# Five weight remainders of VectorE moved to later places in the head loop of a hybrid attention and expert layer

## The chip, the cores and the metric

One Trainium2 chip, one of its cores. The metric is the device time of one execution in microseconds (us), lower is better. The kernel before was timed three times: 2218.05, 2221.12 and 4329.31 us, median 2221.12 us. All operands are float32.

## The reference

One layer on 256 tokens of width 2048. The part that matters here is the first third: an RMS norm, one wide input projection, and three mixers of eight heads of width 128 each, all read from that projection.

```python
xn = rms_norm(x, mix_norm[i])
proj = xn @ w_in[i]
(aq, ak, av, bq, bk, bv, c_qkv, c_a, c_b, c_z, g_a, g_b, g_c) = jnp.split(proj, split_at, axis=-1)
out_a = sliding_window_sink_attention(...)   # softmax over two chunks of 64, with a sink
out_b = stick_breaking_attention(...)        # blocks of 128
# out_c: gated delta rule in chunks of 64. The inverse of (I - N) by squaring:
for _ in range(int(math.log2(CHUNK)) - 1):
    power = power @ power
    t_mat = t_mat + t_mat @ power
# then a recurrence over the chunks: v_new = u - w @ state; state = state * decay + k^T v_new
```

Behind it come the gates and the branch projections (merged output, then `w_out`), a mixture of 32 experts with top-2 routing, and a gated per-layer embedding.

## The kernel before, in words

**Weights in two parts.** Every float32 product with a large weight is done in three passes of fp32r matmuls. ScalarE rounds a landed weight tile to its high part (`wh = copy(slot)`, in `hi`), VectorE computes the remainder (`wl = slot - wh`, in `lo`, line 1332 in the heads and line 1529 for the units of the gate stage), and TensorE adds `wh·xh`, `wh·xl` and `wl·xh`. `lo` begins with a wait for its `hi` (semaphore `w_hi`) and ends by raising `v_lo`.

**Tiles and slots.** A head needs eight tiles of the projection (q, k, v of the delta net, v, q, k of stick-breaking, z of the delta net, q of the window attention), each 2048 x 128, 1 MB. Four slots of the ring hold them. The sync engine issues the load of tile t+4 into the slot of tile t once TensorE has finished tile t (`tile_mm`, line 306). `wl` overwrites the slot in place, `wh` has its own four buffers.

**The head loop.** While head n is mixed, TensorE computes the tiles of head n+1. This is written out by hand: `mix(m, n, dense)` on TensorE (line 529) calls `dense(q)` for q = 0 to 31 between the small matmuls of the mixing; four calls make a tile of 48 matmuls, 12 in a call (`bank<-xh,wh`, `xl,wh`, `xh,wl` in the rows, line 492). The third pass, which needs `lo` of its tile, starts at the ninth matmul of the third call of a tile (wait at line 489). Tile s is thus `dense(4s)` to `dense(4s+3)`. The loop runs seven times; the eighth head is mixed after it with the first units of the gates in place of the tiles, where `lo(2)`, `lo(3)`, `lo(5)`, `lo(6)` and `lo(9)` do units 2, 3, 4, 5, 6 and 7, and `lo(4)`, `lo(7)` and `lo(8)` nothing.

**Order on TensorE around the change.** After `dense(12)` it waits for the softmax weights (`sw_pr`) and transposes them (line 591). Then six rounds r = 0 to 5 of the inverse: `dense(13+r)`, the last matmul of which is held until VectorE and ScalarE have copied the results of the round before (`dn_round`, `dn_roundp`), then small matmuls of 64x64 (lines 600, 603 or 605, and 610). Then `dense(19)`, lines 626 and 628, `dense(20)`, line 632 (the off-diagonal block, `dn_x`), `dense(21)`, line 637 (first half of the new values, which needs the copied block, `dn_inv`), line 638, `dense(22)`, `dense(23)`, line 642 (needs the first half copied, `dn_vn`), `dense(24)`, `dense(25)`, line 648 (needs the state copied), `dense(26)`, `dense(27)`, line 654 (needs the second half copied), and `dense(28)` to `dense(31)`.

**Order on VectorE.** `mix` (from line 1418) is one in-order queue. The lines of the change: the minimum for stick-breaking (1471), the sum, reciprocal and products of the softmax weights (1473 to 1478), the round copies (1482, 1484; 1488 in the last round) each with a tap of the next head's convolution behind it in rounds 0 to 3 (1407, 1409), the product with z (1495), the copy of the off-diagonal block (1497), of the first half of the new values (1500), the SiLU of the next head (1415), the copy of the state (1503) and of the second half (1506). These short steps stand between `lo(2)` to `lo(9)`. `lo(4)` to `lo(7)` make the remainders of the tiles 4 to 7 of the next head, `lo(8)` and `lo(9)` those of the tiles 0 and 1 of the head after it.

**Order on ScalarE.** Round copies of the other operand of the squaring (`dn_roundp`), with `hi(5)` ahead of the rounds, `hi(6)` behind the copy of round 3, the sigmoids of z and of the convolution behind the copy of round 4, `hi(7)` behind the copy for line 638, `hi(8)` behind `evac(5)` after it. In the last head `hi(5)` and `hi(6)` round units 4 and 5.

Of the kernel before, what the change touches and what calls it, by code (L numbers as in the profile page):

```python
# [81 lines left out]
def hybrid_trunk(nc, x, p, mix_norm, w_in, swa_q_norm, swa_k_norm, swa_sinks, sb_q_norm, sb_k_norm, dn_conv,  # L82
# [3 lines left out]
    with ctx:  # L86
# [22 lines left out]
        def sem(name):  # L109
            name = base.get(name, (name, 0))[0]  # L110
            if name not in sems:
                sems[name] = ctx.enter_context(nc.semaphore(name))
            return sems[name]

        def event(name, n):

            name, before = base.get(name, (name, 0))
            return sem(name), n + before
# [861 lines left out]
        def bc(ap, shape):  # L980
            return ap.to_broadcast(shape)
# [321 lines left out]
        def _(dve):  # L1303
            tt, ts, stt = dve.tensor_tensor, dve.tensor_scalar, dve.scalar_tensor_tensor

            def nxt():

                dve.drain()  # L1308
# [20 lines left out]
            def lo(p, t):  # L1329

                dve.wait_ge(*event("w_hi", t + 1))
                tt(wl[p][:], slot[p], wh[p][:], ALU.subtract).then_inc(sem("v_lo"), 1)  # L1332
# [84 lines left out]
            def mix(n, next_tap, next_silu, lo):  # L1417
                one = ds(n - 1, 1)
                dve.drain()
                dve.tensor_copy(hs[:], head[:, 0:F_CONV, one].rearrange("p f a -> p (f a)"))  # L1420
                dve.tensor_copy(v_sw, vt_sw[:, ds((n - 1) // 4, 1), :].rearrange("p a s -> p (a s)"))
                nxt()

                dve.wait_ge(*event("sb_rt", n))
                stt(qk_sb[:, 0:S], raw_sb[:, 0, :], gains[:, 5:6], r_sb[:, 0:S], ALU.mult, ALU.mult)
                stt(qk_sb[:, S:2 * S], raw_sb[:, 1, :], gains[:, 3:4], r_sb[:, S:2 * S], ALU.mult, ALU.mult)\
                    .then_inc(sem("sb_qk"), 1)
                dve.wait_ge(*event("dn_rt", n))
                stt(qk_dn[:, 0:S], cv[:, 0:S], HS, r_dn[:, 0:S], ALU.mult, ALU.mult)
                tt(qk_dn[:, S:2 * S], cv[:, S:2 * S], r_dn[:, S:2 * S], ALU.mult).then_inc(sem("dn_qk"), 1)  # L1430

                G = Gb[:, one, :].rearrange("p a s -> p (a s)")
                for t in range(TT):
                    i = stt(decT[:, t * P:t * P + P], G[:, t * P:t * P + P], hs[:, F_NGC + t:F_NGC + t + 1], capdn,
                            ALU.add, ALU.min)
                i.then_inc(sem("dn_diff"), 1)
                lo(2)
                dve.wait_ge(*event("sw_rt", n))
                stt(q_sw, raw_sw, gains[:, 6:7], r_sw, ALU.mult, ALU.mult).then_inc(sem("sw_q"), 1)

                dve.wait_ge(*event("sb_ln", n))
                stt(sp, bank[3][:, 0:384], 0.0, za, ALU.max, ALU.add)
                nxt()
                spd = sp.rearrange("p (b n) -> p b n", b=3)[:, 0:3:2, :]
                tt(spd, spd, bc(upper[:].unsqueeze(1), [P, 2, P]), ALU.mult).then_inc(sem("sb_sp"), 1)
                lo(3)

                dve.wait_ge(*event("sw_s", n))
                tt(smx, bank[4][:, 0:384], masksw[:].rearrange("p b n -> p (b n)"), ALU.add)
                nxt()  # L1450
                dve.tensor_reduce(sm[:, 0:1], smx[:, 0:P], AX.X, ALU.max)
                dve.tensor_reduce(sm[:, 1:2], smx[:, P:3 * P], AX.X, ALU.max)
                nxt()
                ts(sm[:, 2:4], sm[:, 0:2], hs[:, F_SINK:F_SINK + 1], -1.0, ALU.max, ALU.mult).then_inc(sem("sw_max"), 1)

                dve.wait_ge(*event("dn_dec", n))
                dve.wait_ge(*event("dn_kk", n))
                tt(attnT, bank[7][:, S:2 * S], decT, ALU.mult)
                tt(decT, bank[7][:, 0:S], decT, ALU.mult)
                nxt()  # L1460
                tt(nT, decT.rearrange("p (t n) -> p t n", t=TT), nBb[:, one, :].rearrange("p a (t n) -> p (a t) n", t=TT),
                   ALU.mult).then_inc(sem("dn_round"), 1)
                nxt()
                for i, rows_ in enumerate(BLOCKS):
                    tt(powT[rows_, :, 1, :], nT[rows_, :, CH * i:CH * i + CH],
                       bc(ident[rows_, CH * i:CH * i + CH].unsqueeze(1), [CH, TT, CH]), ALU.add)
                dve.wait_ge(*event("dn_eg", n))
                tt(eG, eG, qk_dn[:, P:S], ALU.mult).then_inc(sem("decays_used"), 1)
                lo(4)
                dve.wait_ge(*event("sb_arg", n))  # L1470
                tt(am, bank[3][:, 0:384], capsb[:].rearrange("p b n -> p (b n)"), ALU.min).then_inc(sem("sb_amin"), 1)
                dve.wait_ge(*event("sw_exp", n))
                tt(sm[:, 8:10], sm[:, 4:6], sm[:, 6:8], ALU.add)
                nxt()
                dve.reciprocal(sm[:, 10:12], sm[:, 8:10])
                nxt()
                ts(smx[:, 0:P], smx[:, 0:P], sm[:, 10:11], None, ALU.mult)
                ts(smx[:, P:3 * P], smx[:, P:3 * P], sm[:, 11:12], None, ALU.mult).then_inc(sem("sw_pr"), 1)
                for r in range(6):
                    dve.wait_ge(*event("dn_sqr", 6 * n - 5 + r))  # L1480
                    if r < 5:
                        i = dve.tensor_copy(powT[:, :, 0, :], pow_psum[:, :, 0, :])
                        if r:
                            i = tt(powT[:, :, 1, :], pow_psum[:, :, 1, :], powT[:, :, 1, :], ALU.add)  # L1484
                        i.then_inc(sem("dn_round"), 1)
                    else:
                        for j, rows_ in enumerate(BLOCKS):
                            i = tt(inv[rows_, :, CH * j:CH * j + CH], pow_psum[rows_, :, 1, :], powT[rows_, :, 1, :], ALU.add)
                        i.then_inc(sem("dn_T"), 1)
                    if r < 4:  # L1490
                        next_tap(r)
                    if r in (1, 3):
                        lo(5 + r // 2)
                dve.wait_ge(*event("z_sig", n))
                tt(ez, ez, raw_z, ALU.mult).then_inc(sem("dn_sz"), 1)
                dve.wait_ge(*event("dn_x", n))
                dve.tensor_copy(inv[BLOCKS[0], :, CH:P], x_psum).then_inc(sem("dn_inv"), 1)
                lo(7)
                dve.wait_ge(*event("dn_v", 2 * n - 1))
                dve.tensor_copy(vn[:, 0:P], bank[6][:, 0:P]).then_inc(sem("dn_vn"), 1)  # L1500
                next_silu()
                dve.wait_ge(*event("dn_ds", n))
                dve.tensor_copy(state, bank[2][:, S:S + P]).then_inc(sem("dn_state"), 1)
                lo(8)
                dve.wait_ge(*event("dn_v", 2 * n))
                dve.tensor_copy(vn[:, P:S], bank[6][:, P:S]).then_inc(sem("dn_vn"), 1)
                dve.wait_ge(*event("dn_ort", n))
                tt(r_dn[:, 0:S], r_dn[:, 0:S], ez, ALU.mult)
                nxt()
                stt(outs[:, 2, one, :].rearrange("p a s -> p (a s)"), bank[4][:, 0:S], gains[:, 4:5], r_dn[:, 0:S],  # L1510
                    ALU.mult, ALU.mult).then_inc(sem("head"), 1)
                lo(9)
# [11 lines left out]
            with dve.Fori(1, NH) as h:  # L1524
                mix(h, lambda j: tap(j, h + 1), lambda: silu(h + 1), lambda s: lo(s % PAIRS, 8 * h + s + PRO))
# [5 lines left out]
            def first_units(s):  # L1531
                for u in {2: (2,), 3: (3,), 5: (4,), 6: (5,), 9: (6, 7)}.get(s, ()):
                    unit_lo(u)

            mix(NH, lambda j: None, lambda: None, first_units)

            def prod(i):
# [278 lines left out]
```

## Time and profile before

| | |
|---|---|
| runs | 2218.05, 2221.12, 4329.31 us; median 2221.12 |
| profiled execution | 2226.76 us, its span 2224.6 us |
| mean granted TensorE clock | 0.936 |
| TensorE busy | 1822.3 us, 82% of the span |
| VectorE busy | 893.1 us, 40% |
| ScalarE busy | 691.5 us, 31% |
| DMA queue of the sync engine | 592.19 MB, 71.5% of 16 engines |

Stages, in us from the start of the span: up to 138.5 the norms, the first tiles and the masks; 138.5 to 643.2 the seven turns of the head loop; 643.2 to 700 the last head; 700 to 1075 gates and branches; to 1215 the output projection and the router; to the end the experts and the embedding. In the seven turns TensorE is busy 456.9 of 504.7 us and the DMA engines 43% of the time; in the last stage the DMA engines are busy 95%.

How to read it: a row of the timeline gives the start, the time taken, the engine, the line and the operation, how many in a row, and in brackets how long the engine had been idle before it and who released it. Matmuls are pipelined, so that a row begins before the one ahead of it has ended: distances are best taken from start to start.

### The profile page before, as it was taken

Reading aid. Unit: us, or ns where it says so; the run is one execution under the profiler, and the core shown is the slowest. Engines: PE = TensorE matmul, PEld = TensorE weight load, DVE = VectorE, ACT = ScalarE, POOL = GpSimd, SP = SyncE. Lnnn points to the kernel's source line nnn. Section 1 sums busy time; section 2 is a strip of 40 time slices with the busy share of each in tenths; the row PEclk is TensorE's granted clock in tenths of the full one; section 3 lists DMA queues with packets and bytes.
Section 4 is the critical chain, followed back from the end, with each engine's and each line's share of the span. In section 5 each row is a group of like instructions: output and inputs, shape, how many; then the busy total and the mean of one; then the engine's idle time right before and its main releaser. Section 6 shows DMA issues by size and latency. Waiting matters only on the chain.

```text
span 2224.6 us, 42071 instructions
## 1 busy us (share of the span) xinstructions
PE 1822.3 (82%) x17850; PEld 1371.7 (62%) x17851; DVE 893.1 (40%) x1420; ACT 691.5 (31%) x952; POOL 26.4 (1%) x40
## 2 busy tenths in 40 slices
PE   5999889999988999999896776666666666666799
PEld 5888888888866888888774443333333333333367
DVE  2464455445544454544443233222222222222274
ACT  3355446554554333333332111001001101011063
POOL 4000000000000000000000000000000000000000
PEclk8999999999998999999998999988988998988899
DMA  8454434544423556555675999999999999999972
GB/s 160 131 135 115 127 98 113 132 113 111 115 94 114 190 189 197 191 197 189 259 274 236 415 427 425 426 426 425 426 426 427 426 427 426 426 427 425 426 273 101
DMA packets 258897, 593.00 MB, mean 267 GB/s; under 512 B 31514, under 2 KB 171034, under 8 KB 225306
## 3 DMA queue, kind: packets, MB, share of 16 engines
q1 hardware_dynamic: 258842, 592.19, 71.5%
q8 instruction: 43, 0.70, 0.1%
q14 instruction: 12, 0.10, 0.0%
HBM read 590.07 MB, written 2.10 MB: 266 GB/s over the span
## 4 chain that ended last, share of the span: by engine, by line
PE 49%; DMA 33%; ACT 6%; DVE 4%; issue 3%; SPq 2%; DVEq 1%; ACTq 1%
DMA ring<-in_w_e_down 32%; PE bank L694 21%; PE bank L492 11%; PE bank L875 4%; PE bank L933 4%; ACT wh L987 3%; PE bank L848 2%; DVE wl L1332 2%; ACT ring L987 2%; SPq L296 1%; DVEq L1308 1%; ACT L987 1%; PE bank L834 1%; DMA ring<-in_w_in 1%; PE bank L894 1%
## 5 line engine op out<-in xcount | busy, mean ns | idle before, releaser
L987 ACT ACTIVATE wh<-ring 128x2048 fp32r<-128x2048 f32 x156 | 298.3, 1912 | 255.4 <-DMA ring<-in_w_in 130.8
L848 PE MATMUL bank<-ring,mo 128*32 128x128 f32 x6144 | 215.2, 300 | 138.5 <-DMA ring<-in_w_e_up 116.5
L848 PEld LDWEIGHTS bank<-ring,mo 128*32 128x32 f32 x6144 | 186.6, 121 | 182.1 <-DMA ring<-in_w_e_up 146.0
L1529 DVE TENSOR_TENSOR wl<-ring,wh 128x2048 fp32r<-128x2048 f32 x86 | 197.2, 2293 | 237.2 <-ACT wh L987 237.1
L987 ACT ACTIVATE mo<-bank 128x128 f32<-128x128 f32 (+2 forms) x145 | 47.7, 335 | 649.3 <-PE bank L862 310.3
L875 PE MATMUL bank<-ring,mo 128*32 128x512 f32 x1024 | 164.0, 772 | 89.4 <-DMA ring<-in_w_e_down 84.6
L1332 DVE TENSOR_TENSOR wl<-ring,wh 128x2048 fp32r<-128x2048 f32 x68 | 155.4, 2287 | 57.5 <-ACT wh L987 57.5
L492 PE MATMUL bank<-xh,wh 128*128 128x256 f32 x1088 | 168.1, 304 | 3.5 <-ACT xh L987 3.5
L492 PE MATMUL bank<-xl,wh 128*128 128x256 f32 x1088 | 161.6, 296 | 3.9 <-POOL xl L448 3.9
L1698 DVE TENSOR_TENSOR x_tok<-x_tok,bank 128x512 f32<-128x512 f32 x256 | 158.2, 680 | 0.0
L492 PE MATMUL bank<-xh,wl 128*128 128x256 f32 x1088 | 148.9, 286 | 6.8 <-DVE mo L1484 6.8
L492 PEld LDWEIGHTS bank<-xh,wh 128*128 128x128 f32 x1088 | 144.7, 199 | 12.6 <-issue 5.3
L492 PEld LDWEIGHTS bank<-xl,wh 128*128 128x128 f32 x1088 | 145.6, 199 | 7.3 <-POOL xl L448 4.2
L875 PEld LDWEIGHTS bank<-ring,mo 128*32 128x32 f32 x1024 | 34.0, 126 | 185.1 <-DMA ring<-in_w_e_down 94.7
L492 PEld LDWEIGHTS bank<-xh,wl 128*128 128x128 f32 x1088 | 137.6, 192 | 8.6 <-DVE mo L1484 8.2
L1708 DVE COPY mo<-bank 128x512 f32<-128x512 f32 x32 | 22.1, 692 | 238.7 <-PE bank L834 238.7
L1722 DVE TENSOR_TENSOR mo<-mo,bank 128x128 f32<-128x128 f32 x32 | 9.2, 288 | 270.5 <-PE bank L848 270.5
L987 ACT ACTIVATE raw_dn<-bank 128x512 f32<-128x512 f32 (+1 forms) x56 | 28.0, 500 | 252.2 <-PE bank L875 245.4
L694 PE MATMUL bank<-wh,xl 128*128 128x512 f32 x384 | 100.6, 401 | 5.0 <-DVE mo L1484 5.0
L694 PE MATMUL bank<-wh,xh 128*128 128x512 f32 x384 | 98.8, 397 | 2.5 <-ACT ring L987 2.3
L987 ACT ACTIVATE ring<-bank 128x128 f32<-128x128 f32 (+6 forms) x132 | 47.8, 378 | 168.3 <-PE bank L610 56.9
L987 ACT ACT_TABLE_LOAD x66 | 84.7, 1283 | 44.4 <-issue 43.2
(352 smaller groups left out, 2319.1 us busy)
## 6 DMA issues: line engine op xcount, KB each, us to landing
ring<-in_w_e_down SPq DMA_DIRECT2D x64, 2048.0 KB, 26.1
ring<-in_w_e_up SPq DMA_DIRECT2D x64, 2048.0 KB, 26.3
ring<-in_w_in SPq DMA_DIRECT2D x116, 1024.0 KB, 5.5
ring<-in_w_e_gate SPq DMA_DIRECT2D x32, 2048.0 KB, 30.6
xnT<-in_w_e_gate SPq DMA_DIRECT2D x16, 2048.0 KB, 29.9
mo<-in_w_e_gate SPq DMA_DIRECT2D x16, 2048.0 KB, 34.2
ring<-in_w_out SPq DMA_DIRECT2D x16, 1024.0 KB, 5.3
ring<-in_w_ple_gate SPq DMA_DIRECT2D x8, 2048.0 KB, 15.3
```

Source lines behind the costliest of these rows:

```text
L296: sp.dma_start(to, of).then_inc(sem("small_in"), 16)
L492: m = mm(to, w_[:, k, :], x_[:, k, :], start=(i == 0), stop=(i == len(steps) - 1))
L694: m = mm(to[t][:], x_(k0 + k, t), w_[p][:, k, :], start=(first and j < 8 and k == 0), stop=(last and j >= 16 and k == 3))
L834: m = mm(bank[0][32 * j:32 * j + 32, :], selw[:, t, :], h_rows[:, t, 512 * j:512 * j + 512], start=(t == 0), stop=(t == 1))
L848: m = mm(bank[b][32 * j:32 * j + 32, 0:P], xw[:, 8 * (i % 2) + k, :], m_gu[piece][:, k, j * P:j * P + P], start=(i % 2 == 0 and k == 0), s ...
L875: m = mm(bank[3][32 * j:32 * j + 32, :], hT[:, 32 * c:32 * c + 32], m_down[i][:, 0, a, j * 512:j * 512 + 512], start=(c == 0), stop=(c == 3))
L894: m = mm(bank[t][:], kT_sw[:, j, t * P:t * P + P], wpp[:, j, ds(n * 512, 512)], start=(j == 0), stop=(j == 1))
L933: m = mm(bank[ACC_BANK[u // 2] + t][:], x_[:, 8 * (u % 2) + k, t * P:t * P + P], w_[:, k, :], start=(first and k == 0), stop=(last and k = ...
L987: return act.activation(out, in_, func, **kw)
L1332: tt(wl[p][:], slot[p], wh[p][:], ALU.subtract).then_inc(sem("v_lo"), 1)
L1529: tt(ul[u % PAIRS], unit_slot[u % PAIRS], uh[u % PAIRS], ALU.subtract).then_inc(sem("u_lo"), 1)
L1698: i = tt(o, o, bank[4 + j][:], ALU.add)
```

## The change

In `mix` of VectorE five calls of `lo` move. `lo(4)` goes from ahead of the stick-breaking minimum to behind the softmax weights. `lo(5)` and `lo(6)` leave the rounds 1 and 3 of the inverse: `lo(5)` goes behind the product with z, `lo(6)` to the place of `lo(7)`, behind the copy of the off-diagonal block. `lo(7)` goes to the place of `lo(8)`, behind the copy of the state, and `lo(8)` behind the copy of the second half of the new values. Their order among themselves, what they compute, and every other engine's program stay.

```diff
                 tt(eG, eG, qk_dn[:, P:S], ALU.mult).then_inc(sem("decays_used"), 1)
-                lo(4)
                 dve.wait_ge(*event("sb_arg", n))
...
                 ts(smx[:, P:3 * P], smx[:, P:3 * P], sm[:, 11:12], None, ALU.mult).then_inc(sem("sw_pr"), 1)
+                lo(4)
                 for r in range(6):
...
                     if r < 4:
                         next_tap(r)
-                    if r in (1, 3):
-                        lo(5 + r // 2)
                 dve.wait_ge(*event("z_sig", n))
                 tt(ez, ez, raw_z, ALU.mult).then_inc(sem("dn_sz"), 1)
+                lo(5)
                 dve.wait_ge(*event("dn_x", n))
                 dve.tensor_copy(inv[BLOCKS[0], :, CH:P], x_psum).then_inc(sem("dn_inv"), 1)
-                lo(7)
+                lo(6)
                 dve.wait_ge(*event("dn_v", 2 * n - 1))
                 dve.tensor_copy(vn[:, 0:P], bank[6][:, 0:P]).then_inc(sem("dn_vn"), 1)
                 next_silu()
                 dve.wait_ge(*event("dn_ds", n))
                 dve.tensor_copy(state, bank[2][:, S:S + P]).then_inc(sem("dn_state"), 1)
-                lo(8)
+                lo(7)
                 dve.wait_ge(*event("dn_v", 2 * n))
                 dve.tensor_copy(vn[:, P:S], bank[6][:, P:S]).then_inc(sem("dn_vn"), 1)
+                lo(8)
                 dve.wait_ge(*event("dn_ort", n))
```

## Rows read from the trace of the kernel before

**Rows 1.** Waits of TensorE in the head loop: total us, times, longest us

```profile
PE bank L591 <- DVE ring L1478: 18.9, 7, 2.7
PE bank L642 <- DVE mo L1500: 12.8, 7, 1.8
PE bank L492 <- DVE mo L1484: 6.8, 7, 1.0
PE bank L541 <- ACT ring L987: 6.6, 7, 1.6
```

**Rows 2.** Timeline of the fifth turn, around the softmax weights

```profile
439.02 2.28 DVE L1332 TENSOR_TENSOR wl<-ring,wh 128x2048 fp32r<-128x2048 f32 x1
441.23 0.55 DVE L1471 TENSOR_TENSOR ring<-bank,capsb 128x384 f32<-128x384 f32 x1
...
442.36 0.35 DVE L1478 TENSOR_SCALAR ring<-ring,sm 128x256 f32<-128x256 f32 x1
...
442.76 0.55 PE L591 MATMUL bank<-ident,ring 128*128 128x128 f32 x3 [2.69 <-DVE ring L1478]
...
445.39 0.29 DVE L1482 COPY mo<-bank 128x128 f32<-128x128 f32 x1 [2.68 <-PE bank L610]
```

**Rows 3.** Timeline of the fifth turn, rounds 3 to 5 of the inverse

```profile
451.46 1.92 PE L492 MATMUL bank<-xh,wh 128*128 128x256 f32 x12
...
456.36 2.29 DVE L1332 TENSOR_TENSOR wl<-ring,wh 128x2048 fp32r<-128x2048 f32 x1 [0.25 <-ACT wh L987]
456.56 1.22 PE L492 MATMUL bank<-xl,wh 128*128 128x256 f32 x8
...
456.68 0.28 ACT L987 ACTIVATE ring<-bank 128x128 f32<-128x128 f32 x1 [0.36 <-PE bank L610]
...
458.27 0.42 ACT L987 ACTIVATE mo<-mo 128x256 f32<-128x256 f32 x1
...
459.10 0.38 PE L492 MATMUL bank<-xh,wl 128*128 128x256 f32 x1 [0.96 <-DVE mo L1484]
459.42 0.45 PE L605 MATMUL bank<-mo,ring 64*64 64x64 f32 x8
459.79 1.70 PE L492 MATMUL bank<-xh,wl 128*128 128x256 f32 x12
```

**Rows 4.** Timeline of the fifth turn, from the block to the first half

```profile
463.65 0.44 PE L632 MATMUL bank<-ring 64*64 64x64 f32 x4
...
465.56 0.39 PE L637 MATMUL bank<-mo 128*128 128x128 f32 x2
...
466.38 1.91 ACT L987 ACTIVATE wh<-ring 128x2048 fp32r<-128x2048 f32 x1
...
468.32 2.29 DVE L1332 TENSOR_TENSOR wl<-ring,wh 128x2048 fp32r<-128x2048 f32 x1 [3.91 <-ACT wh L987]
...
470.87 0.49 PE L642 MATMUL bank<-mo,ring 128*128 128x128 f32 x2 [1.83 <-DVE mo L1500]
```

**Rows 5.** Windows: length, busy us (count) of PE, PEld, DVE, ACT, POOL; clock, DMA

```profile
442.76:459.42 16.66, 15.69 (x164) 14.10 (x164) 11.31 (x24) 9.18 (x17) 0.00 (x0) 1.00 0.28 73
514.89:533.05 18.16, 17.19 (x163) 15.32 (x163) 11.31 (x24) 9.29 (x16) 0.00 (x0) 0.91 0.26 68
544.51:547.93 3.42, 3.42 (x28) 3.42 (x29) 3.21 (x3) 0.39 (x1) 0.00 (x0) 1.00 1.04 285
470.87:475.79 4.92, 4.92 (x29) 4.92 (x30) 3.21 (x3) 0.39 (x1) 0.00 (x0) 0.65 0.72 198
673.50:683.90 10.40, 10.37 (x38) 7.20 (x39) 1.58 (x5) 0.65 (x2) 0.00 (x0) 0.52 0.01 2
708.00:1060.00 352.00, 349.35 (x1554) 289.19 (x1552) 171.03 (x103) 135.62 (x91) 0.00 (x0) 1.00 0.59 192
```

**Rows 6.** Timeline of the last head, round 4 of the inverse

```profile
670.66 0.26 ACT L987 ACTIVATE ring<-bank 128x128 f32<-128x128 f32 x1
...
673.53 0.79 PE L694 MATMUL bank<-wh,xl 128*128 128x512 f32 x1 [5.05 <-DVE mo L1484]
```

## The prediction, as it was written before the changed kernel ran

> **What bounds the kernel now.** I read the windows first. The change touches only the head loop and the last head, 138.5 to 700 us of the span, and there TensorE is nearly always busy while VectorE and the DMA engines are not half so. So I asked the waits of TensorE in the loop what its gaps are [rows 1]: the reader is to see that the three longest are all for VectorE, seven times each, once a turn: 2.7 us for the softmax weights, 1.8 us for the first half of the new values, 1.0 us for a round of the inverse. The fourth, for ScalarE's inverse root, is no part of the change. Then the timeline of one turn shows what VectorE does just before it releases TensorE, and each time it is a remainder of 2.28 or 2.29 us, which nobody needs yet [rows 2 to 4]. Last, windows of the same stretches in different turns show what the gaps do to TensorE's clock [rows 5], and the last head is read apart [rows 6]. All starts below are those of the fifth turn; the gaps repeat to 0.02 us in the other six.
>
> **The change part by part.** Nothing is computed anew: eight remainders a turn before and after. Each term is a gap of TensorE that ends earlier.
>
> *lo(4), ahead of the minimum.* VectorE starts it at 439.02, the minimum at 441.23, and the softmax weights are done at 442.36 + 0.35 = 442.71, 1.48 us after the minimum began [rows 2]. TensorE has been idle since 442.76 - 2.69 = 440.07. With the remainder gone the minimum starts at 439.02, the weights are there at 440.50, and TensorE starts at 440.54: 0.47 us of the gap stays, 2.22 us go. Behind the weights the remainder runs from about 440.4 to 442.7. What is next on VectorE's queue is the copy of round 0, at 445.39 now, 443.17 then, and it was idle 2.68 us ahead of it [rows 2]: 0.5 us of cover is left, so this place costs nothing; without the cover it would delay round 0, whose result TensorE holds its twelfth matmul for, over a microsecond later. ScalarE's exponential of the minimum only comes earlier.
>
> *lo(5), in round 1.* It ends 1 us into the next stretch of twelve matmuls and holds back the last of it: that stretch takes 1.92 us where one after 64-wide matmuls takes 1.70 when nothing holds it [rows 3]. 0.22 us go.
>
> *lo(6), in round 3.* It waits for `hi(6)`, starts at 456.36, and the copies of round 4 come after it. TensorE's twelve matmuls start at 456.56 and line 605 at 459.42: 2.86 us, of which 0.96 is a gap and the rest of the surplus the slow restart. Not held, they take 1.63 to the next start (0.07 less than the 1.70 of the row at 459.79, whose end overlaps what follows). ScalarE's copy for the same round is there at 456.96, so it does not take VectorE's place. 2.86 - 1.63 = 1.23 us go.
>
> *lo(5) in its new place* starts behind the product with z. That one needs the sigmoid, done at 458.27 + 0.42 = 458.69 less the 0.22 from above [rows 3], and the copies of round 5, which end about 1.1 us after line 605; line 605 starts at 456.56 - 0.22 + 1.63 = 457.97. So the product ends at 459.5, the remainder at 461.7. The block that VectorE must copy next comes out of line 632, which starts 4.23 us after line 605 [rows 3, 4], hence at 462.2, and ends at 462.6. 0.9 us of cover: cost nothing. If the cover were gone, the copy could still be 1.3 us late before line 637, a dozen matmuls on, waits.
>
> *lo(6) in its new place* runs from 462.9 to 465.1 (`hi(6)` is long done). Line 637 starts 6.14 us after line 605 [rows 3, 4], at 464.1, so VectorE copies the first half at 465.1 to 465.4, about 0.9 us later than it could. Line 642 waits for it. It could have started at 470.87 - 1.83 = 469.04 [rows 4], 9.62 us after line 605, in the new turn at 467.6. 2.2 us of cover, cost nothing.
>
> *lo(7), ahead of the first half.* It had to wait for `hi(7)`, which starts at 466.38, because that stands behind line 638 on ScalarE; it starts at 468.32 and makes line 642 late by 1.83 us, plus a slow first matmul, 0.49 against 0.22 us [rows 4]. 2.10 us go. Behind the state's copy it finds `hi(7)` done, runs 2.3 us, and the second half comes about 3.0 us after that copy: 0.7 us of cover, and then 24 matmuls before line 654 needs the copy of it. *lo(8)* behind that copy has nothing queued behind it but the output, for which VectorE idles for over ten microseconds. Each costs nothing.
>
> *Remainders as TensorE needs them.* The third pass of tile 5 starts 16 matmuls ahead of the end of `dense(23)`, 2.1 us before 467.6; lo(5) is done at 461.7, 3.8 us ahead. The others have 7 us or more. No DMA is issued by VectorE, and the loads of the sync queue wait for TensorE's tiles, not for remainders; they are shifted with the tiles.
>
> Sum of a turn: 2.22 + 0.22 + 1.23 + 2.10 = 5.77 us; times seven, **40.4 us**.
>
> *The clock.* In some turns TensorE runs for 3.4 us at the lower of its two levels (1.2 in place of 2.4 GHz) right after one of the two long gaps. From line 591 to 605 a turn takes 16.66 us at a granted clock of 1.00 and 18.16 at 0.91; from 642 to 648 it is 3.42 at 1.00 and 4.92 at 0.65 [rows 5]. Five turns have it in the first stretch and three in the second: 8 x 1.50 = 12.0 us. It comes back if the gaps of 2.69 and 1.83 us are what lowers the clock. For that speaks that none of the eight comes after the gap at line 541, 6.6 / 7 = 0.9 us [rows 1], and that the gates, without such gaps, run 352 us at 1.00 [rows 5]. Bounds: nothing comes back, or all of it does. I take all of it, since gaps of 0.5 and 0.9 us are what remains. The Trainium skill has a rule against this ("TensorE: Matmul & The Clock Gate", A second HAM failure mode): short idle times between groups of matmuls, if frequent, make the clock swing between its levels. By it the small gaps that remain would keep the stretches, and the sum would be 12 us less.
>
> *The last head.* lo(5) and lo(6) are units 4 and 5 there. TensorE is idle 5.05 us until VectorE's round 4, behind the remainder of unit 5. ScalarE's copy for that round is itself behind `hi` of unit 5, which waits for its load, and is done at 670.92 [rows 6]. So the gap ends at about 671.0 and not at 673.53: 2.5 us go. The next 10.4 us run at 0.52 [rows 5], 5.1 us dearer than at full clock; between none and all of it I take a third, 1.7 us, since half the gap stays. Together **4.2 us** (2.5 to 7.6).
>
> All of it: 40.4 + 12.0 + 4.2 = 56.6 us. The profiled execution took 2226.76 us, its span 2224.6, so it would be 2170.2. The median of the runs is 5.6 us lower; 2221.12 - 56.6 = 2164.5, taken as **2165 us**, -2.5%.
>
> **The rivals.** *A, the clock keeps swinging* (the skill's rule; 0.13). For it: its low stretches are short and stand wherever a turn has gaps. Against: rows 5. The eight stretches and the last head's stay: 2165 + 12.0 + 1.7 = 2179 us.
>
> *B, a moved remainder becomes a new wait* (0.14). The tightest places have 0.5 (round 0) and 0.9 us (the block) of cover, and VectorE is one queue. If the block's copy or round 0 ends up behind a whole remainder in each turn, TensorE waits at line 637 or in `dense(14)`: up to 2.3 us x 7 = 16 us back, 2181 us.
>
> *C, the remainders come too late for the third pass* (0.03), the case on the slower side. Its place is the wait at line 489; its price is the whole remainder exposed, 5 x 2.29 x 7 = 80 us, less the 57: 2244 us. It decides only once lo(5) is more than 3.8 us later than I have it and the others over 7. Against it: every `hi` stands unchanged on ScalarE, and is done before the new place.
>
> *D, the gain is given back later* (0.05): the experts are bound by the DMA engines, and would absorb what comes sooner if their loads ran on a clock of their own: 2221 us. Against: their first loads wait for units of the output projection, so they shift with TensorE. That the change does not do what it says is in the same 0.05: the calls are the same on one in-order queue, so I see no way to it.
>
> **How the numbers follow.** Forecast 2165 us with 0.65. Its own spread is 2150 (all of the last head's clock, the fastest run of 2218 as the base, and the scatter of a run) to 2176 (half of the clock). Range 2150 to 2186, which takes in A, B and a part of both together; C, D and the tails are left out, under 0.2. A difference of 2% (44 us, about what a measurement can tell) means below 2177. Forecast 0.62, a third of A and a quarter of B: 0.70 faster. Within 2%: 0.28. Slower by over 2%: 0.02, as even C stays at +1%.
>
> **What would show it.** In the trace after: the gap at line 591 about 0.5 us; no gap at line 642 and none at line 492 released by 1484; a turn of 64.5 to 65 us in place of 72.1; clock 1.00 in the loop; 2.5 us of gap in the last head's round 4. The prediction is wrong if TensorE waits at 637 or 489, if the copy at 1482 of round 0 starts right on the end of a remainder with TensorE held, if the clock still shows eight stretches at half, or if the experts start no earlier than 50 us before.

## The result, and the profile after

The changed kernel takes 2167.64 us (median of 4 runs, 2164.89 to 2171.17) against 2220.61 us before: a ratio of 0.9766, 95% interval 0.9746 to 0.9787, faster. One of the four runs of the kernel before took 4329.31 us and is not in the ratio. Forecast were 2165 us and 2150 to 2186. The profiled execution took 2164.89 us, its span 2162.8.

The waits of TensorE in the seven turns of the head loop and the start of the last head (total us, times, longest us), which answer to [rows 1]:

```profile
PE bank L541 <- ACT ring L987: 5.0, 6, 0.8
PE bank L591 <- DVE ring L1477: 3.4, 7, 0.5
PE bank L534 <- ACT ring L987: 1.2, 1, 1.2
```

The rows for line 642 and for the rounds are gone, the one for 591 has 0.5 us a turn in place of 2.7, and ScalarE's is as it was: 0.84 us in six of the seven turns. The seventh wait of [rows 1], 1.6 us long, belongs to the last head, which this window leaves out; the prediction's mean of 0.9 us mixes the two. Lines of VectorE's `mix` from 1470 to 1504 have moved up or down by one in places: 1470 is the minimum, 1477 the last of the softmax weights, 1496 the block's copy, 1499 the copy of the first half, 1502 that of the state.

The timeline of the fifth turn, which answers to [rows 2]:

```profile
407.92 0.55 DVE L1470 TENSOR_TENSOR ring<-bank,capsb 128x384 f32<-128x384 f32 x1
...
409.05 0.35 DVE L1477 TENSOR_SCALAR ring<-ring,sm 128x256 f32<-128x256 f32 x1
...
409.31 2.28 DVE L1332 TENSOR_TENSOR wl<-ring,wh 128x2048 fp32r<-128x2048 f32 x1
409.45 0.55 PE L591 MATMUL bank<-ident,ring 128*128 128x128 f32 x3 [0.48 <-DVE ring L1477]
...
412.08 0.29 DVE L1482 COPY mo<-bank 128x128 f32<-128x128 f32 x1 [0.49 <-PE bank L610]
```

The remainder is now behind the weights, and the copy of round 0 still finds VectorE idle, for 0.49 us (forecast 0.5). The rounds and the block, which answer to [rows 3] and [rows 4]:

```profile
418.15 1.70 PE L492 MATMUL bank<-xh,wh 128*128 128x256 f32 x12
...
423.03 1.22 PE L492 MATMUL bank<-xl,wh 128*128 128x256 f32 x8
...
424.09 0.64 PE L492 MATMUL bank<-xh,wl 128*128 128x256 f32 x4
424.66 0.45 PE L605 MATMUL bank<-mo,ring 64*64 64x64 f32 x8
...
426.12 2.28 DVE L1332 TENSOR_TENSOR wl<-ring,wh 128x2048 fp32r<-128x2048 f32 x1
...
429.37 0.28 DVE L1496 COPY mo<-bank 64x128 f32<-64x128 f32 x1 [0.97 <-PE bank L632]
429.58 2.27 DVE L1332 TENSOR_TENSOR wl<-ring,wh 128x2048 fp32r<-128x2048 f32 x1
...
431.78 0.28 DVE L1499 COPY mo<-bank 128x128 f32<-128x128 f32 x1
...
434.12 0.39 PE L642 MATMUL bank<-mo,ring 128*128 128x128 f32 x2
```

From 423.03 to line 605 (424.66) it is 1.63 us, where it was 2.86. The block's copy has 0.97 us of cover (forecast 0.9), and line 642 no longer waits. Windows of the same stretches as in [rows 5], lines 591 to 605, then 642 to 648, of the last head behind its round 4, and of the gates:

```profile
409.45:424.66 15.21, 15.21 (x164) 13.97 (x164) 9.21 (x23) 7.96 (x15) 0.00 (x0) 1.00 0.47 128
434.12:437.44 3.32, 3.32 (x30) 3.32 (x29) 2.49 (x2) 2.19 (x2) 0.00 (x0) 1.00 0.54 152
618.00:626.90 8.90, 8.90 (x38) 6.10 (x39) 5.89 (x7) 2.14 (x4) 0.00 (x0) 0.62 0.00 0
650.00:1000.00 350.00, 348.73 (x1551) 288.79 (x1549) 170.02 (x102) 135.68 (x91) 0.00 (x0) 1.00 0.58 192
```

The granted clock is 1.00 in the whole loop. In the last head round 4 now waits for ScalarE:

```profile
617.51 0.26 ACT L987 ACTIVATE ring<-bank 128x128 f32<-128x128 f32 x1
...
617.91 0.48 PE L694 MATMUL bank<-wh,xl 128*128 128x512 f32 x1 [1.89 <-ACT ring L987]
```

The two traces side by side, by the starts of the matmul of line 534 at the head of each turn, of line 660 at the end of the last head, and of the span:

| stretch | before | after | difference |
|---|---|---|---|
| up to the first line 534 | 130.40 | 129.66 | -0.7 |
| seven turns, to the last line 534 | 504.06 | 452.01 | -52.05 |
| last head, to its line 660 | 56.42 | 52.13 | -4.3 |
| from there to the end | 1533.7 | 1529.0 | -4.8 |

The last row is none of the change: in fourteen traces of this study it lies between 1529.0 and 1534.6 us, whatever the kernel. The loop and the last head make 56.4 us, the medians 53.0 us; the scatter of the rest explains a difference of this size, and with the medians of the later comparisons (before 2221.54 to 2222.82, changed kernel 2171.8 once more) it is 50 to 55.

### The profile page after: what moved, and what is told of

It reads as the page before. It is cut to its first block, busy times and chain, and to the rows that moved or that the text cites. A ratio compares the mean times of both kernels' runs of the same rounds, so it can differ in the third digit from the quotient of the medians.

```text
span 2162.8 us, 42071 instructions
## 1 busy us (share of the span) xinstructions
PE 1805.4 (83%) x17850; PEld 1360.0 (63%) x17851; DVE 894.0 (41%) x1420; ACT 691.1 (32%) x952; POOL 26.4 (1%) x40
## 4 chain that ended last, share of the span: by engine, by line
PE 52%; DMA 34%; ACT 5%; DVE 3%; SPq 2%; issue 2%; DVEq 1%; ACTq 1%
DMA ring<-in_w_e_down 33%; PE bank L694 21%; PE bank L492 12%; PE bank L875 4%; PE bank L933 4%; ACT wh L987 2%; PE bank L848 2%; ACT ring L987 2%; SPq L296 1%; DVEq L1308 1%; ACT L987 1%; DVE wl L1332 1%; PE bank L603 1%; PE bank L834 1%; DMA ring<-in_w_in 1%
## 5 line engine op out<-in xcount | busy, mean ns | idle before, releaser
L492 PE MATMUL bank<-xh,wh 128*128 128x256 f32 x1088 | 162.7, 298 | 2.1 <-ACT xh L987 2.1
L492 PE MATMUL bank<-xl,wh 128*128 128x256 f32 x1088 | 157.0, 291 | 3.4 <-POOL xl L448 3.4
L492 PEld LDWEIGHTS bank<-xl,wh 128*128 128x128 f32 x1088 | 141.0, 193 | 6.8 <-POOL xl L448 3.7
L694 PE MATMUL bank<-wl,xh 128*128 128x512 f32 x384 | 97.3, 394 | 0.0
```

Source lines behind the costliest of these rows:

```text
L492: m = mm(to, w_[:, k, :], x_[:, k, :], start=(i == 0), stop=(i == len(steps) - 1))
L694: m = mm(to[t][:], x_(k0 + k, t), w_[p][:, k, :], start=(first and j < 8 and k == 0), stop=(last and j >= 16 and k == 3))
```

## The experiments

Three kernels make one part of the change alone, two undo one part, three stretch a gap or a cover, and three go on from the changed kernel. For each the length of the loop is read from its trace like in the table above, with the number of low stretches in it. A low stretch is 3.4 us of TensorE at the lower of its two clocks; two in a row count as two.

| kernel | median us (ratio to before, interval) | loop us | low stretches |
|---|---|---|---|
| before | 2220.61 | 504.06 | 8 |
| changed | 2167.64 (0.9766, 0.9746 to 0.9787) | 452.01 | 0 |
| only lo(4) | 2195.22 (0.9877, 0.986 to 0.9893) | 476.72 | 0 |
| only the rounds | 2203.46 (0.9918, 0.9902 to 0.9935) | 489.45 | 5 |
| only lo(7), lo(8) | 2202.42 (0.9906, 0.9889 to 0.9922) | 484.63 | 5 |
| all but lo(4) | 2190.92 (0.9867, 0.9848 to 0.9887) | 476.91 | 7 |
| all but the rounds | 2180.04 (0.9813, 0.9795 to 0.9831) | 462.09 | 0 |
| gap of 1.1 us | 2171.76 (0.9769, 0.9751 to 0.9787) | 456.41 | 0 |
| gap of 1.75 us | 2178.01 (0.9802, 0.9783 to 0.9821) | 460.95 | 0 |
| cover taken | 2175.64 (0.9786, 0.9767 to 0.9804) | 456.31 | 0 |
| lo(3) too | 2158.86 (0.9714, 0.9699 to 0.9728) | 447.79 | 0 |
| dense(5) earlier | 2170.47 (0.977, 0.9753 to 0.9786) | 455.37 | 0 |
| both | 2163.86 (0.9738, 0.9722 to 0.9754) | 451.27 | 0 |
| changed, again | 2171.8 (0.977, 0.9754 to 0.9786) | 452.01 | 0 |

**Only lo(4).**

```diff
-                lo(4)
                 dve.wait_ge(*event("sb_arg", n))
...
                 ts(smx[:, P:3 * P], smx[:, P:3 * P], sm[:, 11:12], None, ALU.mult).then_inc(sem("sw_pr"), 1)
+                lo(4)
```

> Only lo(4) moves, the other four stay where they were before the change. Theory (each gap of TensorE is a term of its own, and the low clock stretches follow the gaps): the gap at line 591 falls from 2.69 to 0.49 us, 2.2 us x 7 = 15.5 us; the gap of 1.83 us at line 642 and that of 0.96 us in round 4 stay; of the eight low stretches (5 after line 591, 3 after line 642) the five after 591 go, but some more may now follow line 642, so 15.5 plus 0 to 7.5 us: 2197 to 2205 us against 2220.6. Rival (the stalls hand over to each other, so that only the whole change pays): the time gained at 591 is lost again at round 4 or 642, whose gaps grow: 2215 to 2221 us. Rival on the clock (it swings whatever the gaps): eight low stretches as before, 2205 us.

Measured 2195.22 us, better than the best end of the expectation. Its waits, and the window of the loop:

```profile
PE bank L642 <- DVE mo L1500: 12.8, 7, 1.8
PE bank L492 <- DVE mo L1484: 6.8, 7, 1.0
PE bank L541 <- ACT ring L987: 5.1, 6, 0.8
PE bank L591 <- DVE ring L1477: 3.4, 7, 0.5
```

```profile
128.20:604.90 476.70, 446.64 (x3795) 415.81 (x3793) 255.66 (x459) 270.53 (x445) 0.00 (x0) 1.00 0.46 123
```

The other two gaps are exactly what they were before, so nothing is handed over. And all eight low stretches are gone, the three behind line 642 too, though its gap stands: the loop is 27.3 us shorter, 2.2 x 7 + 8 x 1.5 = 27.4.

**Only the rounds.**

```diff
                     if r < 4:
                         next_tap(r)
-                    if r in (1, 3):
-                        lo(5 + r // 2)
...
                 tt(ez, ez, raw_z, ALU.mult).then_inc(sem("dn_sz"), 1)
+                lo(5)
...
                 dve.tensor_copy(inv[BLOCKS[0], :, CH:P], x_psum).then_inc(sem("dn_inv"), 1)
+                lo(6)
                 lo(7)
```

> Only lo(5) and lo(6) move out of the rounds (lo(6) directly ahead of lo(7), which stays ahead of the first half of the new values). Theory: 0.22 + 1.23 = 1.45 us a turn, 10.2 us, and the last head's 2.5 us and up to 1.7 of its clock; both long gaps stay and with them about eight low stretches: 12.5 to 14.5 us, 2206 to 2208 us. Rival (stalls hand over): the gap at line 642 grows by as much as the rounds get shorter; only the last head's 2.5 to 4 us remain, 2217 us.

Measured 2203.46 us, 2.5 us below the expectation. The gap at 642 is 1.83 us as before, against the rival. The loop is 14.6 us shorter: 1.45 x 7 = 10.15, and three low stretches fewer than before, 4.5, which the theory had not counted.

**Only lo(7) and lo(8).**

```diff
                 dve.tensor_copy(inv[BLOCKS[0], :, CH:P], x_psum).then_inc(sem("dn_inv"), 1)
-                lo(7)
...
                 dve.tensor_copy(state, bank[2][:, S:S + P]).then_inc(sem("dn_state"), 1)
-                lo(8)
+                lo(7)
                 dve.wait_ge(*event("dn_v", 2 * n))
                 dve.tensor_copy(vn[:, P:S], bank[6][:, P:S]).then_inc(sem("dn_vn"), 1)
+                lo(8)
```

> Only lo(7) and lo(8) move behind the state and the second half; lo(4), lo(5), lo(6) stay as before. Theory: the gap of 1.83 us at line 642 and the slow restart go, 2.1 us x 7 = 14.7 us; the three low stretches behind line 642 go, those behind line 591 stay and may become seven: 14.7 plus 1.5 to 4.5 us: 2201 to 2206 us. Rival (stalls hand over): 2215 to 2221 us. Rival on the clock (it swings whatever the gaps): stretches at half clock still begin behind line 642.

Measured 2202.42 us, as the theory has it. The loop is 19.4 us shorter: 2.10 x 7 + 3 x 1.5 = 19.2. The five low stretches left are all at line 591: three begin up to 1.4 us behind the end of its gap and two within the gap.

With 1.5 us for each low stretch taken off, the three parts gain 27.3 - 12.0 = 15.3, 14.6 - 4.5 = 10.1 and 19.4 - 4.5 = 14.9 us, together 40.3, where the whole change has 52.05 - 12.0 = 40.05. The gaps add up. The low stretches do not: the three kernels have eight, three and three fewer than before, and there were eight.

**All but lo(4).** The changed kernel with `lo(4)` back ahead of the minimum (the first diff, reversed).

> The whole change but for lo(4), which stays ahead of the minimum. Theory: the gap at line 591 is back at 2.69 us, 15.4 us more than the changed kernel, and low stretches come back behind it in some or all of seven turns, 0 to 10.5 us: 2183 to 2194 us against 2167.6. If the clock does not hang on the gaps, no low stretch comes back and the time is 2183 us. If the parts were not additive, the difference to the changed kernel would be under 10 us.

Measured 2190.92 us, within. The loop is 24.9 us longer than in the changed kernel: 15.4 for the gap of 2.69 us, and 9.5 for low stretches at line 591 again, in six of the seven turns: five of 3.4 us and one of 6.8, counted as seven. Five of the six begin within the gap:

```profile
PE bank L591 <- DVE ring L1478: 18.8, 7, 2.7
PE bank L541 <- ACT ring L987: 5.1, 6, 0.9
```

```profile
129.20:606.10 476.90, 450.92 (x3796) 423.40 (x3794) 256.79 (x459) 271.25 (x445) 0.00 (x0) 0.97 0.46 123
```

**All but the rounds.** The changed kernel with `lo(5)` and `lo(6)` back in rounds 1 and 3.

> The whole change but for lo(5) and lo(6), which stay in rounds 1 and 3. Theory: 1.45 us a turn come back, 10.2 us, and the last head's 4.3 us: 14 to 15 us more than the changed kernel, 2182 us, with a gap of 0.96 us ahead of line 605 and, since gaps under 1 us have shown no low stretch, none in the loop. Rival (gaps of about 1 us, frequent, are enough to lower the clock): low stretches of 3.4 us in the turns, up to 10 us more, 2185 to 2192 us.

Measured 2180.04 us. The loop is 10.08 us longer (10.15 expected), the clock 1.00, and the last head takes 55.6 us in place of 52.1. The low stretches that the rival would have in the loop are not there.

**The gap, in two lengths.** One more minimum with a drain ahead of the real one, and then two:

```diff
                 dve.wait_ge(*event("sb_arg", n))
+                tt(am, bank[3][:, 0:384], capsb[:].rearrange("p b n -> p (b n)"), ALU.min)
+                nxt()
```

> The changed kernel with one more minimum and a drain (0.6 us) on VectorE ahead of the softmax weights, writing what it writes anyway: the gap at line 591 goes from 0.49 to about 1.1 us. Theory: 0.6 x 7 = 4.3 us more than the changed kernel, 2172 us, no low stretch. Rival (frequent short gaps lower the clock): low stretches appear, 2173.5 to 2182 us.

> The same with two more minimums and drains (1.25 us): the gap at line 591 goes to about 1.7 us, close to the 1.83 us that stood at line 642 before. Theory: 1.25 x 7 = 8.7 us, and low stretches in some turns (0 to 7, 1.5 us each), 2176 to 2187 us. If the clock hangs on the length of the gap alone between 1.1 and 1.7 us, this kernel shows stretches and the one with 0.6 us more shows none.

Measured 2171.76 and 2178.01 us. The waits of the second, and its window of the loop:

```profile
PE bank L591 <- DVE ring L1481: 12.3, 7, 1.8
PE bank L541 <- ACT ring L987: 6.6, 7, 1.6
```

```profile
128.90:589.80 460.90, 441.42 (x3795) 414.50 (x3794) 264.56 (x473) 270.99 (x445) 0.00 (x0) 1.00 0.48 128
```

The loop is 4.4 and 8.9 us longer, 0.63 and 1.28 us a turn, as long as what was put in: a microsecond on this stretch of VectorE's queue is a microsecond of the kernel. Neither shows a low stretch in the loop, with gaps of 1.13 and 1.76 us in every turn. (The seventh wait at line 541, 1.6 us, is again that of the last head.)

**The cover.** Four such minimums between `lo(5)` and the block's copy, about as long as one more remainder:

```diff
                 lo(5)
+                for _ in range(4):
+                    tt(am, bank[3][:, 0:384], capsb[:].rearrange("p b n -> p (b n)"), ALU.min)
+                    nxt()
                 dve.wait_ge(*event("dn_x", n))
```

> The changed kernel with four more minimums and drains (about 2.5 us, as long as one remainder) on VectorE between lo(5) and the copy of the off-diagonal block. Theory: VectorE was idle 0.97 us there and the copy may come 1.3 us late before line 637 waits, so TensorE loses 0.2 to 0.4 us a turn, 1 to 3 us in all, 2169 to 2171 us, and the first half of the new values is not late. Rival (the cover is only VectorE's idle time of 0.9 us, what goes beyond it is lost): 1.6 us a turn, 11 us, 2179 us.

Measured 2175.64 us. In the fifth turn:

```profile
427.14 0.45 PE L605 MATMUL bank<-mo,ring 64*64 64x64 f32 x8
...
430.92 2.46 DVE L1496 TENSOR_TENSOR ring<-bank,capsb 128x384 f32<-128x384 f32 x4
...
433.45 0.28 DVE L1499 COPY mo<-bank 64x128 f32<-64x128 f32 x1
433.66 2.27 DVE L1332 TENSOR_TENSOR wl<-ring,wh 128x2048 fp32r<-128x2048 f32 x1
433.79 0.49 PE L637 MATMUL bank<-mo 128*128 128x128 f32 x2 [0.34 <-DVE mo L1499]
```

2.46 us more on VectorE cost TensorE a gap of 0.34 us. Start to start, line 637 comes 6.65 us behind line 605 in place of 6.14, and line 638 another 0.10 us later: the loop is 4.3 us longer, 0.61 us a turn. So the place holds 2.46 - 0.51 = about 2.0 us before TensorE feels it, 0.97 of them idle time of VectorE, where the theory had 0.97 + 1.3. The cost lies above the theory (0.2 to 0.4 us a turn) and far below the rival (1.6). Rival B of the prediction needed a whole remainder of delay here; even that would have taken back 4 us and not 16. The median rose by some 4 us more than the loop; 1.5 of them are in the last head (53.6 us), and the rest is scatter of the stretch behind it (1534.5 us in this trace, 1529.0 in that of the changed kernel).

**Three variants of the changed kernel.** The first moves `lo(3)` off the chain as well, the second asks TensorE to do `dense(5)` ahead of line 541, where it waits for ScalarE, the third does both.

```diff
                 tt(spd, spd, bc(upper[:].unsqueeze(1), [P, 2, P]), ALU.mult).then_inc(sem("sb_sp"), 1)
-                lo(3)
...
                 ts(smx[:, P:3 * P], smx[:, P:3 * P], sm[:, 11:12], None, ALU.mult).then_inc(sem("sw_pr"), 1)
-                lo(4)
+                lo(3)
...
                     if r < 4:
                         next_tap(r)
+                    if r == 0:
+                        lo(4)
```

```diff
                 dense(4)
+                dense(5)
                 pe.wait_ge(*event("dn_sq", n))
                 pe.wait_ge(*event("sb_rt", n))
                 mm(bank[2][:], ones[:], sq_dn, start=True, stop=True).then_inc(sem("dn_ss"), 1)
-                dense(5)
```

> The changed kernel, and lo(3) goes from ahead of the window attention's scores to behind the softmax weights, lo(4) from there to behind the tap of round 0. Theory: VectorE's chain to the softmax weights starts on the scores and not on the end of a remainder, 0.5 to 0.6 us earlier, so the gap of 0.49 us at line 591 goes, with its slow restart of up to 0.2: 3.4 to 5 us; in the last head the 2.98 us gap at line 586 shrinks to about 0.7: 2.3 us. 2160 to 2162 us against 2167.6. Rival (lo(4) behind round 0 delays the copies of round 1, which TensorE then waits for; or the third pass of tile 3 waits for its remainder): 2166 us or more.

> The changed kernel with dense(5) on TensorE moved ahead of the sum of squares at line 541, for which TensorE waits 0.84 us a turn. Theory (the chain from there over ScalarE and VectorE to the softmax weights has no slack left, as VectorE is just in time at line 591): the gap at 541 goes and the one at 591 grows from 0.49 to about 1.8 us; 2167 to 2171 us. Rival (gaps are independent terms): 0.84 x 7 = 5.9 us and about 1 in the last head, 2161 us.

> Both of these. Theory: with lo(3) out of the chain there are about 0.6 us of slack, so the gap at 541 goes and that at 591 stays at 0.2 to 0.6 us: 1.1 us a turn or 0.8 at least, 6 to 8 us, and 2 to 3 us in the last head: 2157 to 2160 us. Rival (independent terms): 0.49 + 0.84 us a turn, 9.3 us, and 3 in the last head, 2155 us.

> The changed kernel itself once more, beside the three variants of it on the same chip: 2165 to 2171 us, no low stretch in the seven turns, turns of 64.9 us.

The first is the fastest kernel here, 2158.86 us beside 2171.8 for the changed kernel on the same chip (run again: a little above its expectation, with the loop of 452.01 us as before). Its fifth turn:

```profile
402.66 0.56 DVE L1448 TENSOR_TENSOR ring<-bank,masksw 128x384 f32<-128x384 f32 x1 [1.52 <-PE bank L575]
...
407.76 2.28 DVE L1332 TENSOR_TENSOR wl<-ring,wh 128x2048 fp32r<-128x2048 f32 x1
...
411.80 2.29 DVE L1332 TENSOR_TENSOR wl<-ring,wh 128x2048 fp32r<-128x2048 f32 x1
...
414.00 0.28 DVE L1481 COPY mo<-bank 128x128 f32<-128x128 f32 x1
```

VectorE waits for the scores now, TensorE waits in the loop for ScalarE at line 541 alone, and the copy of round 1, 0.4 us late behind `lo(4)`, holds nobody. The loop is 4.2 us shorter and the last head 2.9, 7.1 together, within the expected sum of 5.7 to 7.3; the median is 1.1 us below the expected 2160 to 2162. Medians differ by 12.9 us, which is more than the traces show; the spans of the two profiled executions by 6.9. I take 7 us as the effect.

The second brings no gain, 2170.47 us, but not in the way I had it:

```profile
PE bank L545 <- ACT ring L987: 9.2, 6, 1.5
PE bank L591 <- DVE ring L1477: 3.3, 7, 0.5
```

The wait moved on to line 545, one step down, and grew from 0.84 to 1.53 us: ScalarE's next inverse root starts on line 541's result. It never came to line 591, whose gap is unchanged. The loop is 3.4 us longer, 455.37 us; the last head, 50.1 us, is 2.0 shorter, with one low stretch fewer. The third is 2163.86 us, slower than both of its expectations (2157 to 2160, and 2155): its loop of 451.27 us is that of the first with the loss of the second, 3.5 us.

## Why the prediction was right

*The gaps.* The term for lo(4) was 2.22 us a turn and a gap of 0.47 left: in the trace 0.48. For the rounds 1.45: 10.1 / 7 = 1.44 by the two kernels that make or undo that part alone. For line 642 2.10, with all of the gap gone: 14.9 / 7 = 2.13. (Its "0.49 against 0.22 us" set the length of a pair of matmuls against a distance from start to start; like with like it is 0.49 against 0.39, or 0.32 against 0.23. The size of the term was right all the same.) The sum of 5.77 us a turn stands against (52.05 - 12.0) / 7 = 5.72. It held since each gap ended on a VectorE instruction that directly followed a remainder, and since the covers of 0.5 and 0.9 us ahead of the new neighbours were read right: 0.49 and 0.97.

*The clock.* 12.0 us were forecast to come back and did: the loop has no stretch at the lower level. The attribution, five stretches to the gap of 2.69 us and three to that of 1.83, is left open. The kernel with only lo(4) moved keeps the seven gaps of 1.83 and has none. That looks as if all eight hung on the gap of 2.69, but it does not show it: gaps of one length are now followed by a stretch and now not, and the kernel with only the rounds moved keeps all fourteen long gaps and has five stretches in place of eight.

So the moment at which a gap falls decides too. The low stretches of one trace begin whole stretch lengths apart; counted on from them, the four gaps of 1.83 us with a stretch (in the kernel before and the one with only the rounds) ended 2.0 to 3.2 us behind such a point and the ten without one 0.05 to 1.6. All seven of the kernel with only lo(4), whose turns repeat to 0.01 us but for the first and the last, ended 0.15 to 1.15 us behind one, where none of the others was followed by a stretch either. Likewise 2.69 us: the eight without a stretch ended 1.3 to 1.8 us behind such a point, the twenty with one before or after that part. The return of all 12.0 us is measured; which share the gap of 1.83 alone would have kept is not.

Rival A is refuted for gaps of 0.5 to 1.76 us: the loops with them run at 1.00, and the gaps of 1.76 us ended at moments from 0.5 to 3.4 us, those included at which gaps of 1.83 had a stretch. The Trainium skill's rule that frequent short idle times make the clock swing ("TensorE: Matmul & The Clock Gate", A second HAM failure mode) is not borne out by these gaps.

*The last head.* 4.2 us were forecast, 4.3 measured, and the close match is in part luck. The gap of 5.05 became 1.89 and not 2.5 us, as from line 591 on the rounds ahead of it took 0.3 us longer and unit 5 could be rounded 0.35 us sooner than before; the low stretch behind round 4 shrank from 10.2 to 6.8 us. Neither size is steady: with lo(5) and lo(6) still in the rounds, three other traces have a gap of 4.1 to 4.2 us there and a last head of 53.8 to 55.6 us, and with lo(4) alone undone, which changes nothing in the last head, it takes 50.6 in place of 52.1.

*Rivals.* B did not happen. Of its two places one was stretched, the block: it holds about 2.0 us and not only its 0.97 of idle time. Round 0 was not tried. C did not arise: no row of line 492 waits for a remainder. D neither: the stretch from the last head to the end takes 1529.0 us in the changed kernel and 1533.7 before, so nothing was given back there.

*The total.* The trace gives 56.4 us for what the change touches against 56.6 forecast; the medians give 53.0. Runs of one kernel differ by more than this (2164.89 to 2171.17 us). 2165 us was 2.6 us low.

## What to carry to other kernels

When an in-order queue releases the busiest engine, look at the instruction just ahead of the releasing one, and ask who needs its result and when. Work with a late due time belongs behind each release and not ahead of it; its new place costs nothing as long as the next release has cover, which is the idle time of the queue ahead of it plus what the waiting engine still has to do. Gaps that end on the same engine may be summed if each is fed by its own late step; a wait fed by a chain that begins at the previous wait, as lines 541 and 545 here, only moves.

## What the runs showed of the hardware

Idle gaps of TensorE of 2.69 us came with a stretch of about 3.4 us at half clock in 5, 4, 5 and 6 of seven turns of four kernels. The stretch began between 0.7 us ahead of the end of the gap and 1.4 us behind it, and cost 1.5 us in the kernel before. Gaps of 0.5 to 1.76 us, once or several times a turn, were never followed by one in the loop of any of the fourteen traces. Gaps of 1.83 us had one in three turns of the kernel before and one turn of another, both with the gap of 2.69 us too, and in none of the seven turns of the kernel that has them without it; as those seven fell at nearly the same moment, they count for little more than one. After a gap the first matmuls are slow even at full clock: the two of line 642 took 0.49 us behind one and 0.39 us without, and start to start with line 643 0.32 against 0.23 us. A third of the change's gain in the loop is thus in no row of waits: 12.0 of the 52.05 us are clock, and some 5 the restarts and the held matmul of round 2.
